# A decoder trunk on eight cores: the output projection runs block by block with all its weights on chip, and the residual and the next norm of a block are queued under the next block's projection

## What is computed

```python
for i in range(2):
    h = rmsnorm(x, g_pre_mix[i])
    # layer 0: retention, 6 heads; layer 1: forgetting attention, 12 heads; both: 4 memory heads
    mixed = jnp.concatenate([self_out, mem_out], axis=-1)      # (B, S, 1024)
    x = x + rmsnorm(mixed @ w_out[i], g_post_mix[i])           # output projection, residual
    h = rmsnorm(x, g_pre_mlp[i])                               # the "next norm"
    u = jax.nn.relu(h @ w_up[i])                               # 1024 -> 4096
    x = x + rmsnorm((u * u) @ w_down[i], g_post_mlp[i])
```

## Time and profile before

| | us |
|---|---|
| median of 3 runs (4429.04 to 4432.4) | 4431.63 |
| the profiled execution's own time | 4432.73 |
| its span, core 1, the slowest | 4431.2 |
| spans of the other cores | 4394.6 to 4426.6 |
| PE busy | 3608.8 (81%) |
| ACT / DVE / POOL busy | 1871.8 / 1564.9 / 800.2 |

### The profile page before, as it was taken

One profiled execution on the slowest core, in us unless ns is written; L12 is line 12 of the kernel. 1 busy time (PEld: TensorE's weight loads), 2 busy tenths in 40 slices (PEclk: granted clock), 3 DMA queues, 4 the chain that ended last, 5 costly groups with the idle time before them and its releaser, 6 DMA issues.

```text
span 4431.2 us, 60029 instructions; the slowest of 8 cores (4394.6 to 4431.2 us)
## 1 busy us (share of the span) xinstructions
PE 3608.8 (81%) x19144; PEld 1677.2 (38%) x19144; DVE 1564.9 (35%) x2613; ACT 1871.8 (42%) x3237; POOL 800.2 (18%) x1050
## 2 busy tenths in 40 slices
PE   2598789996888896999826986999968888869997
PEld 1254234442433432444313532444434343324443
DVE  3564441323322225222136644414232222251322
ACT  2476332222578753222024773313226777532220
POOL 0253121212100002111112631212130000021111
PEclk8698799997999997999957987999979999989998
DMA  5142134443000012546431421445430000124554
GB/s 127 36 86 52 19 60 67 74 67 62 13 13 13 8 18 36 72 69 141 69 109 39 89 46 20 70 67 74 67 55 13 13 11 8 22 43 68 88 91 86
DMA packets 135597, 241.62 MB, mean 55 GB/s; under 512 B 17536, under 2 KB 21632, under 8 KB 135296
## 3 DMA queue, kind: packets, MB, share of 16 engines
q0 software_dynamic: 94176, 171.48, 26.5%
q1 hardware_dynamic: 41120, 66.30, 5.2%
HBM read 367.12 MB, written 16.78 MB: 87 GB/s over the span
## 4 chain that ended last, share of the span: by engine, by line
PE 71%; DVE 8%; issue 6%; ACT 6%; DMA 5%; POOL 2%; SPq 1%; DVEq 0%; ACTq 0%; POOLq 0%
PE pb L989 20%; PE pb L979 18%; PE pb L757 10%; PE pb L965 5%; PE pb L928 4%; PE pb L941 3%; PE pb L782 2%; ACT scrB L1131 2%; DMA wr_s<-wall 2%; POOL xT_s L1510 2%; DVE scrF L1302 2%; PE pb L918 2%; DMA mixT_s<-scrF 2%; PE pb L838 1%; DVE hT_s L1290 1%
## 5 line engine op out<-in xcount | busy, mean ns | idle before, releaser
L979 PE MATMUL pb<-hT_s,wr_s 128*128 128x512 bf16 x4096 | 905.3, 383 | 35.0 <-DMA wr_s<-wall 27.7
L1495 POOL DMA_DIRECT2D wr_s<-wall x623 | 332.8, 534 | 2756.0 <-PE pb L989 795.3
L979 PEld LDWEIGHTS pb<-hT_s,wr_s 128*128 128x128 bf16 x4096 | 403.2, 99 | 535.2 <-issue 67.5
L1131 ACT ACTIVATE scrB<-pb,small_s 128x512 bf16<-128x512 f32 x960 | 535.3, 623 | 153.0 <-PE pb L944 60.3
L1239 ACT ACTIVATE scrB<-pb 128x512 bf16<-128x512 f32 x512 | 305.7, 597 | 624.9 <-PE pb L979 624.9
L989 PE MATMUL pb<-mixT_s,wr_s 128*128 128x512 bf16 x2048 | 478.0, 388 | 0.0
L989 PE MATMUL pb<-u2hi_s,wr_s 128*128 128x512 bf16 x2048 | 454.6, 379 | 0.3 <-DMA wr_s<-wall 0.2
L965 PE MATMUL pb<-scrB,u2hi_s 128*128 128x512 bf16 x960 | 338.8, 356 | 94.8 <-ACT scrB L1131 83.5
L782 PE MATMUL pb<-scrF,cbf_s 128*128 128x512 bf16 x256 | 117.9, 516 | 355.7 <-ACT scrF L1066 354.5
L941 PE MATMUL pb<-rsd,u2hi_s 128*128 128x512 bf16 x960 | 340.6, 360 | 60.3 <-DVE rsd L1457 60.3
L1245 ACT ACTIVATE scrB<-pb 128x512 bf16<-128x512 f32 x128 | 76.3, 597 | 720.0 <-DVE hT_s L1480 719.9
(11 more groups left out here) (155 smaller groups left out, 4160.3 us busy)
## 6 DMA issues: line engine op xcount, KB each, us to landing
wr_s<-wall POOLq DMA_DIRECT2D x623, 256.0 KB, 4.0
mixT_s<-scrF SPq DMA_DIRECT2D x192, 128.0 KB, 2.4
xT_s<-xT SPq DMA_DIRECT2D x8, 2048.0 KB, 18.7
outT<-xT_s SPq DMA_DIRECT2D x8, 2048.0 KB, 9.6
u2hi_s<-wall POOLq DMA_DIRECT2D x31, 256.0 KB, 4.9
u2hi_s<-memT SPq DMA_DIRECT2D x32, 128.0 KB, 6.8
rl_s<-pos SPq DMA_DIRECT2D x8, 256.0 KB, 3.4
rsd<-tab_s SPq DMA_DIRECT2D x96, 1.0 KB, 1.7
```

The source lines that it names most:

```text
L979: ins = pe.matmul(pb[:], lhsT=wu[:, k, :], rhs=hT[:, k, bsl(b)], start=k == 0, stop=k == 7)
L1131: act.activation(out=pt[:, 0:wd], in_=at("fs", s, i)[:, 0:wd], func=AF.Exp, bias=bias, scale=0.125).then_inc(*M.at("fex", (s, i)))
L1495: pool.dma_start(out=buf[slot], in_=wall_d[wall_idx[unit]]).then_inc(*M.at(f"w_{slot}", n, 16))
```

## The change

The output projection's loops are swapped: `b` outside, `oc` inside. All 8 weight units must then be on chip at once, so they get 8 places (`OW`): in layer 0 the lower half of `u2hi`, free after retention, loaded by 8 issues in one go ahead of the memory attention; in layer 1 four places in the key buffer and three in the value buffer of head pair 4, loaded in one go just after pair 5 has begun, and `X2`, which was the ring's fourth slot. The ring `W3` passes straight on to the first up units. Behind the items of a block its `ors` is queued, and for blocks 0 and 1 its 8 tails and the 8 groups of its next norm (list `behind`); after each projection item of the next block, from `oc` 1 on, three entries of that list are issued. The tails of blocks 2 and 3 stay late.

```diff
+OW = (("O0", "O1", "O2", "O3", "O4", "O5", "O6", "O7"), ("O0", "O1", "O2", "O3", "U0", "U1", "U2", "X2"))
 # fox
             P.add("ft", s, i)
+            if i == last[("f", 4)] + AHEAD:
+                P.open(OW[1][:7], ("out", s, 1), ("fpv", (s, last[("f", 4)])))
 # out_proj
-        for oc in range(8):
-            for b in range(NBLK):
+        behind = []
+        for b in range(NBLK):
+            for oc in range(8):
                 P.take(PB, ("op", s, l, oc, b), ("osq", (s, l, oc, b)))
                 P.take(BS, ("osq", s, l, oc, b), ("oss", (s, l, oc, b)))
                 P.add("op", s, l, oc, b)
-            P.weight(W3, ("out", l, oc), s, ("op", (s, l, oc, 3)))
+                if b == NBLK - 1:
+                    P.weight(OW[l], ("out", l, oc), s, ("op", (s, l, oc, 3)))
+                for _ in range(3):
+                    if oc > 0 and behind:
+                        what, *k = behind.pop(0)
+                        if what == "ors":
+                            P.add("ors", *k)
+                        elif what == "tail":
+                            tail(*k)
+                        else:
+                            norm_do(what, *k)
+            behind.append(("ors", s, l, b))
+            if b < 2:
+                behind += [("tail", s, l, 1, b, oc) for oc in range(8)]
+                behind += norm_groups(s, l, 2, b)
+                normed.add((s, l, 2, b))
         P.add("oss", s, l)
-        for b in range(NBLK):
-            P.add("ors", s, l, b)
-        for b in range(NBLK):
+        for what, *k in behind:
+            P.add(what, *k)
+        for b in (2, 3):
             for oc in range(8):
-                if b < 2:
-                    tail(s, l, 1, b, oc)
-                else:
-                    late.append((s, l, 1, b, oc))
+                late.append((s, l, 1, b, oc))
 # make_plan, layer 0
                 retention(s, l)
+                P.open(OW[0], ("out", s, 0), ("ro", (s, 5, 3)), ("gsg", (s, 5, 3)))
                 mem_attn(s, l)
 # buffers
+        for i in range(8):
+            buf[f"O{i}"] = u2hi[:, i * 1024:(i + 1) * 1024]
+        for i in range(3):
+            buf[f"U{i}"] = u2hi[:, 8192 + i * 1024:8192 + (i + 1) * 1024]
```

## The result

| | before | changed |
|---|---|---|
| runs compared, us | 4430.72 (median of 4) | 4397.6 and 4387.1 |
| ratio, 95% interval | | 0.9913 [0.9890, 0.9937] |
| profiled execution, us | 4432.73 | 4397.6 |
| span of the slowest core, us | 4431.2 (core 1) | 4395.9 (core 5) |
| span of core 1, us | 4431.2 | 4384.7 |

The chip ran some executions with a lower TensorE clock on one die or both; a ratio here compares only executions without that, which is why it does not go by the plain median of all. By the ratio the change gains 38.5 us, with an interval of 28 to 49. Measured a second time, beside the last experiments, it was 0.9904 [0.9887, 0.9921].

What follows compares the result with a forecast made beforehand. PE was taken as the bound, winnable only where idle around the output projection: 46 us from the holes less 14 for the clock less 1.5 for weights gives 31, from 4432.7 to 4401.7, as median 4401; range 4372 to 4430.

Steps and rivals of the forecast that it cites:

- The hole and the chain: Around the output projection: 208 us of PE holes, DVE's serial work; queue-order chains in blocks 1 and 2 take 163, leaving 46.
- The clock: Blocks 1 and 2: TensorE likely falls to 1.2 GHz, costing item 5 1.73 us eight times, 14 us; bounds 0 to 41.
- the down projection's row: Profile row in the down projection: 2.80 us of PE idle at clock 1.00, clock 0.50 behind it; the clock term's evidence.
- The tails: Residual additions on DVE in blocks 1 and 2: eight take 10.3 us, 11.6 with two casts between them.
- The weights: Layer 0 loads hidden under memory attention, cost 0; layer 1 loads may delay key rows, 1.5 us taken, at most 12.
- The moved tails: Eight late tails moved from the hole to behind up units: 10.7 us of DVE, covered by the up projection.
- All items cold: Rival, blocks 1 and 2: three chain items per block at 1.2 GHz, gain 3 us, 4428; chance 0.11.
- slower: Rival: clock stays low through the chain items and into block 3, 50 us slower, 4482; chance 0.06.
- late weights: Rival, layer 0: each weight unit takes 8 us instead of 4, the last 14 us late, twice, 4429; chance 0.03.
- free order: Rival, blocks 1 and 2: chain dissolves, only DVE's own sum counts, gain 163 us, 4269; chance 0.05.
- all hidden: Rival, output projection: all queued work hidden except ones-matmuls, gain 195 us, 4237; chance 0.03.
- late rows: Layer 1, pair 5: key rows delayed by weight loads, at most two by 3 us in each of two sequences, 12 us.

Runs made afterwards that it cites:

- Experiment 1: Against the kernel before: only loops swapped and all projection weights resident, `ors`, tails and norms again behind the projection; ratio 0.9992 [0.9968, 1.0016].
- 2: Against the changed kernel: two entries of the list behind issued per item instead of three; ratio to the kernel before 0.9877 [0.9860, 0.9894].
- 5: Against the changed kernel: ones-matmuls of the norm's squares queued on PE behind the next projection item, not ahead; ratio to the kernel before 0.9875 [0.9846, 0.9904].
- 6: Against the changed kernel: ones-matmuls one item later, entries issued two and one in turn over blocks 1 to 3; ratio to the kernel before 0.9691 [0.9663, 0.9719].
- 8: Against the changed kernel: entries issued two and one in turn over blocks 1 to 3, ones-matmuls not moved; one comparable time, 4370.1 us, no ratio.
- 9: Against the changed kernel: six entries issued per item instead of three; one comparable time, 4429.7 us, no ratio.
- experiment 3: Against the changed kernel: extra useless matmuls in PE's idle stretches of blocks 1 and 2; second run's ratio to the kernel before 0.9899 [0.9870, 0.9927].
- experiment 7: Against 6: first squares of the norm placed between the tails; ratio to the kernel before 0.9666 [0.9637, 0.9694], profiled execution 4279.2 us.

## Why the prediction was right

The forecast was 4401, a gain of 31 us; the ratio gives 38.5, and 4387 to 4398 were measured. The mechanism held, and most sizes. That the total comes so near is in part luck: the occurrences gained 44 to 45 us where the forecast had 32 for them (469.3 less 437.5), and some 7 us were lost outside them (see "Open").

**The hole and the chain.** Forecast: the hole goes, blocks 1 and 2 become chains of 35.9 us at full clock plus 1.7 for item 5. Measured: 36.2 and 36.6. By steps, from the rows above (core 5, block 1), each from the end of the one before:

| step | forecast | measured |
|---|---|---|
| 1 cast of item 1 to first tail | 2.9 | 2.9 (476.61 to 479.47) |
| 2 eight tails, two casts | 11.6 | 10.9 (to 490.39) |
| 3 cast and square of item 4 | 1.4 | 1.3 (to 491.65) |
| 4 six squares, last sum | 3.6 | 3.7 (to 495.39) |
| 5 item 5, its cast and square, two squares | 4.5 + 1.7 | 5.4 (to 500.83) |
| 6 to the first product of the norm | 2.1 | 2.3 (to 503.16) |
| 7 eight products, a cast | 6.1 | 5.9 (to 509.07) |
| 8 to item 1 of block 2 and its cast | 3.7 | 3.7 |
| sum | 35.9 + 1.7 | 36.2 |

That the sum at the full clock, 35.9, lies so near 36.2 is chance: the tails were shorter than forecast by what the clock added. PE's waits stood where the prediction said, though some were shorter: 2.78 and 1.37 us before the sums of items 2 and 3 (3 forecast), 4.07 before the first ones-matmul (4), and 0.71 and 1.14 before the sums of items 6 and 7 (2).

Experiment 1 shows that the gain comes from the queued work, 2, 5, 6, 8 and 9 that the order of the queues sets what of it arrives.

**The clock** is the term that was mis-sized. I took 1.73 us for item 5 in each of 8 blocks, 14 us. In the row it is 3.0 from its start to its cast instead of 2.0. Over the eight blocks of core 5 this time goes from 2.3 to 3.7, 8.6 us too long in all, and experiment 3 gives back 9. The clock fell as the down projection's row had suggested, but it rises within an item (8 matmuls in 2.91 us lie between 1.89 and the 3.62 of item 5 in block 2), so an item at the fall or rise pays a part. The rule of the Trainium skill ("TensorE: Matmul & The Clock Gate", section "HAM oscillation — how this bites in real kernels"), that each burst between idle stretches starts cold, fits most of these rows and not all: of the 24 items 4, 5 and 6 on core 5, 7 ran at 1.89 us. What I had hung on it, three full items on the chain, was too much, since items 4 and 6 are hidden behind DVE: their casts wait for the tails and for the products of the norm.

**The tails** cost 0.7 us less per block than forecast, 5 us over 8 blocks. Of that, 0.56 is one addition. In the kernel before, DVE's second addition of a series ran beside POOL's (524.49 to 525.74 in the earlier trace rows) and took 1.25 us:

```profile
525.05 1.25 DVE L1308 TENSOR_TENSOR xT_s<-xT_s,scrF 128x512 f32<-128x512 f32 x1 [0.17 <-DVE scrF L1302]
```

In the changed kernel the cast of item 2 stands ahead of it, POOL's is all but over by then, and it took 0.69 (483.16 above):

```profile
482.01 1.26 POOL L1531 TENSOR_TENSOR xT_s<-xT_s,scrF 128x512 f32<-128x512 f32 x1 [63.97 <-DVE scrF L1323]
```

The prediction had asked only whether POOL's additions could slow the casts. Clock and tails together are about 11 us; the four occurrences on core 5 have 425.4 us, and the forecast was 423.5 + 14 = 437.5.

**The weights** cost nothing in layer 0: POOL issued the eight in one go, and no projection matmul waits for a DMA in any of the four occurrences.

```profile
403.46 1.15 POOL L1563 TENSOR_TENSOR mixT_s<-rsd,scrB 128x512 bf16<-128x512 f32 x1 [3.03 <-DVE rsd L1448]
404.55 4.30 POOL L1516 DMA_DIRECT2D u2hi_s<-wall  x8
```

In layer 1 the first burst landed at a median of 7.9 us per unit (core 5) instead of 4.0, and one key row of pairs 4 and 5 took 5.4 us (core 5) instead of at most 4.1. But PE's longest wait as pair 5 begins is the one of before, 2.86 us for a cast by DVE against 2.85, and none there is for a DMA. So my 1.5 us for it are not seen. The wait of the fourth up unit went too: on core 1 up matmuls wait 15.8 us for weights over the run, against 27.7.

**The moved tails** were covered, as forecast: no gap in the ups from 562.85 to 690.

**The rivals.** All items cold (4428), slower (4482) and late weights (4429) lie above what was measured; free order (4269) and all hidden (4237) below. Free order is the interesting one: experiment 7 comes to 4279, 10 us from it, though by freeing the order and also by passing work on to block 3. One bound of the range was added up wrongly: two cold items per block (28 us) and late rows (12) leave a gain of 6 of the 46, which is 4425 and not 4420. The range reached to 4430 and held either way.

**Open.** On core 1 the occurrences account for the change: 469.3 less 424.0 is 45.3, and its span fell by 46.5. Core 5, the slowest of the changed kernel, has the same occurrences within 1.5 us, but its span fell only 29.8 (4425.7 to 4395.9). Over the eight cores the spans fell by 37 us in the mean and the occurrences by 45. The largest part of the 8 us between, 3.7, lies in the up and down projections behind the second occurrence, where single cores differ by 12 us before the change and by 8 after it. Why was not found; run 1 shows 3 us there too and is no slower than the kernel before.

## What to carry to other kernels

Work hidden under matmuls is worth what the order of the queues lets through, not what the engines' sums allow. With in-order engines, walk the chain from one item to the same item one block later, with each hand-off, before believing in cover; here it predicted 37.6 us, the clock included, for what took 36.2 and 36.6. Then issue the hidden work in small, even portions, and put a reduction's matmul one item behind the operation that feeds it: the same instructions went from a gain of 38 us to one of 137 to 148 (runs 6 and 7), and in larger portions, by one time, to none. The pace of two and one also spreads the work over three blocks instead of two; no run parts that from the small portions, but by DVE's sum it could give 23 us at most.

## What was not expected of the hardware

Two cures of the same chain gave 22 us and 24 to 29 alone and 100 to 102 together, and with them the granted clock in the same window rose from 0.69 to 1.00. PE idle stretches of 0.4 to 1.2 us between items left it at 1.00 in that window; with stretches of 1.4, 1.9, 2.8 and 4.1 us it was at 0.81 over a block. Weight loads issued in one go landed at a median of 7.9 us each (layer 1, core 5) instead of 4.0. The eight of layer 0, issued within 4.3 us, were all on chip 12.9 to 18.1 us after the first issue (cores 1 and 5); one behind the other at 4.0 they would need 32, an estimate from the median of single loads.
